# Moving block loads between issuing queues in a one-layer encoder kernel: staged weight blocks to the sync engine, f loads to GpSimd

## The chip, the core and the metric

One core of a Trainium2 chip runs the whole layer. The metric is device time in microseconds (us) of one execution. A core has TensorE (PE), VectorE (DVE), ScalarE (ACT), GpSimd (POOL) and the sync engine (SP). SP, ACT and POOL can each issue DMAs; each works its program strictly in order, so a wait holds back everything that stands behind it on that engine.

## What is computed

The layer has one combined input projection, three token mixers, a gated merge, an output projection and a squared-ReLU MLP, all in float32 (SEQ 512, D_MODEL 2048):

```python
h = _rmsnorm(x, norm1[l])
proj = jnp.einsum('bsd,de->bse', h, w_in[l])
(u_pool, c_b, c_c, c_x, q, k, v, qi, ki, wi, gate_logits) = jnp.split(proj, pts, axis=-1)
...
merged = (g[:, :, 0] * jnp.einsum('bsp,pd->bsd', a, w_pool_out[l])
          + g[:, :, 1] * jnp.einsum('bsp,pd->bsd', bconv, w_conv_out[l])
          + g[:, :, 2] * jnp.einsum('bsp,pd->bsd', c, w_attn_out[l]))
x = x + jnp.einsum('bsd,de->bse', merged, w_o[l])
h2 = _rmsnorm(x, norm2[l])
f = jnp.square(jax.nn.relu(jnp.einsum('bsd,df->bsf', h2, w_ff1[l])))
x = x + jnp.einsum('bsf,fd->bsd', f, w_ff2[l])
```

## The kernel before

Every float32 operand is split into a high part (rounded, made by ACT) and a low part (the rest, made by DVE), and a product is three matmuls: hi*hi, hi*lo, lo*hi. For the narrow weights the piece of work is a **unit**: 2 tiles of 128 rows by 256 columns. SP loads two units at a time into `w_raw` (512 KB, `load`, L535), ACT makes `w_hi` (`split_hi`, L458), DVE makes `w_lo` (`split_lo`, L465), PE multiplies (L488 to L490, for v L974 to L976). `w_hi` and `w_lo` have four slots, and the splits run three units ahead of PE (`PREFETCH`): turn n of DVE's and ACT's loop handles unit n + 3, whose slot is free when PE has finished unit n - 1.

The order is q and k (64 units, 8 per pass), v (32 units), then the attention with the convolution's weights (48 units). In these stretches something else is prepared on the side: for three large products later on (the gate's first column block, `J` 0, and the output projection's, `J` 6 and 7) Strassen-like sums of weight blocks are needed. A **stage** s (12 of them) loads four 512 KB blocks into `stage` (L2736), DVE mixes them with four subtractions (`mix_stage`, L1960, L1963, L1966, L1969), and each mixed block is stored to `t_dram` (L2741), to be read back later as `block_g` or `block_w`. Stages 0 to 7 share one set of four buffers, stages 8 to 11 another. GpSimd issues both the loads and the stores. It waits for the previous stage's stores to land before it issues the next stage's loads:

```python
if s:
    pool.wait_ge(stage_mixed, 4 * s)
    pool.wait_ge(stage_stored, 64 * s)
```

DVE does the mixes between its splits at fixed turns: in q and k at turns 4 to 7 of each pass of 8 (mixes 0, 1, 2, 3), in v at turns 11 to 14, 18 to 21 and 25 to 28 (stages 8, 9, 10), and stage 11 at turns 3 to 6 of the attention. Mix 0 waits until all four blocks have landed, and the splits of later units stand behind it on DVE.

The MLP's first product is computed 16 times over (`q`, 0 to 15), its squared results f are split and stored by SP to `f_dram` (L768, 256 KB each). The second product (`J` 8 to 15, two passes over each of four chunks of f; 28 turns a pass, its weights loaded by SP as `group`, L600) reads f back into `sf`: `load_s(c, n, freed)` (L1762) waits for the chunk's stores and for PE's last use of the buffer, then issues two 1 MB loads from ACT's queue. ACT's list calls it 28 times, between the splits and evictions that ACT also does.

Of the kernel before, what the change touches and what calls it, by code (L numbers as in the profile page):

```python
# [29 lines left out]
F32 = mybir.dt.float32  # L30
# [32 lines left out]
def build(nc, xT, x, cst_dram, w_in, pool_w, w_po, w_co, w_ao, w_o, w_f1, w_f2, out):  # L63
# [31 lines left out]
    with ctx:  # L95
# [432 lines left out]
        def _(sp):  # L528
# [29 lines left out]
                            sp.dma_start(h_dram[k0:k0 + 4].rearrange("k p c -> p k c"), xin[:, k0:k0 + 4, :]  # L558
                                         ).then_inc(h_spilled, 16)

            with sp.Fori(0, 8) as i:
                for n in range(LP):
                    load(i * LP + (u_qk // 2 + n), n % RAWS, w_in, n * 2 * UK * P, i * COLS + c_q)
            with sp.Fori(0, 4) as i:
                for n in range(LP):
                    load(i * LP + (u_v // 2 + n), n % RAWS, w_in, n * 2 * UK * P, i * COLS + c_v)
            sp.wait_ge(a_lo, NW)
            for hl, part in ((0, br_hi), (1, br_lo)):
                sp.dma_start(br_dram[0:4, hl].rearrange("k p c -> p k c"), part[:, 0:4, :].bitcast(F32)
# [8 lines left out]
            def spill_c(h):  # L578
                sp.wait_ge(c_lo, h + 1)
                for hl, part in ((0, br_hi), (1, br_lo)):  # L580
                    sp.dma_start(br_dram[8 + h, hl], part[:, 8 + h, :].bitcast(F32)).then_inc(c_spilled, 16)
# [38 lines left out]
            for i, col in enumerate((c_c, c_x, c_b, c_c + COLS, c_x + COLS, c_b + COLS)):  # L620
                for n in range(LP):
                    load(u_att // 2 + i * LP + n, n % RAWS, w_in, n * 2 * UK * P, col)
                    l = i * LP + n
                    if l >= 7 and (l - 7) % 3 == 0:
                        spill_c((l - 7) // 3)
                    if l == 15:
                        sp.wait_ge(ab_spilled, 32)
                        for idx in range(4):
                            load_block(0, idx)
                    if l == 17:  # L630
                        spill_b(0)
            spill_c(6)
            sp.wait_ge(pv_mm, ATTN_HEADS)

# [618 lines left out]
        def _(act):  # L1253
# [499 lines left out]
                if q < F1_PAIRS and k == 13:  # L1753
                    square_f(q, 0)

            def load_s(c, n, freed):

                for s in range(PIECES):
                    act.wait_ge(f_spilled[s], 32 * ((28 * (c + 1) - s + PIECES - 1) // PIECES))
                act.wait_ge(g_done, freed)  # L1760
                for h in range(2):
                    act.dma_start(sf[h][n].rearrange("p l k c -> p l (k c)").bitcast(F32),  # L1762
                                  f_dram[c, n, :, :, h * 2 * S:(h + 1) * 2 * S].rearrange("l p c -> p l c")
                                  ).then_inc(s_landed[n], 16)


            hi1(0, 0, 0)
            hi1(0, 1, 0)
# [25 lines left out]
            for q in range(1, F1_PAIRS):  # L1794
                for k in range(14):
                    hi1(q, k // 2, k % 2)
                    act_after(q, k)
                    if q == F1_PAIRS - 1 and k in (5, 7, 9, 11, 13):
                        n = (k - 5) // 2
                        load_s(0, n, 28 * 8 + 14 * q + 2 * n + 2)  # L1800

            for J in range(8, 16):
                it, c = J - 8, (J - 8) // 2
                for idx, (n, g) in enumerate(order_of(J)):
                    hi2(J, n, g)
                    if it == 0 and idx < 14:
                        act_after(F1_PAIRS, idx)
                    if it == 0 and idx in (1, 3):
                        load_s(0, 5 + idx // 2, K2 - 3 + idx)
                    if it % 2 == 1 and c < 3 and idx == 11:  # L1810
                        load_s(c + 1, 0, K2 + 28 * it + 8)
                        load_s(c + 1, 1, K2 + 28 * it + 8)
                    if it % 2 == 1 and c < 3 and idx == 23:
                        for n in (4, 3, 2):
                            load_s(c + 1, n, K2 + 28 * it + 20)
                    if it % 2 == 0 and c and idx == 3:
                        load_s(c, 5, K2 + 28 * it)
                        load_s(c, 6, K2 + 28 * it)


        @block.vector
        def _(dve):
# [149 lines left out]
            for n in range(8 * UP):  # L1972
                split_lo(dve, u_qk + n + PREFETCH, n + PREFETCH)
                if n == 0:
                    pool_group(3)
                if n % UP < 6:
                    t = n % UP % 3
                    chain.step(dve.max(top8[t], work[t][:]))
                    chain.wait()
                    chain.step(dve.match_replace(work[t][:], top8[t], work[t][:], EMPTY))  # L1980
                    chain.wait()
                if n % UP >= 4:
                    mix_stage(n // UP, n % UP - 4)


            def mask(t):
# [20 lines left out]
            for n in range(4 * UP):  # L2007
# [28 lines left out]
                    chain.wait()  # L2036
                if n == 24:
                    diagonals(dve, rqk, 32, dk)
                if 11 <= n < 29 and (n - 11) % 7 < 4:
                    mix_stage(8 + (n - 11) // 7, (n - 11) % 7)  # L2040


            def landed(J, place):
# [662 lines left out]
        @block.gpsimd  # L2706
        def _(pool):

            for kt in range(KT):
                pool.wait_ge(x_squared, kt + 1)  # L2710
                if kt == 0:
                    pool.tensor_copy(dg[:, :], sq[:, 0]).then_inc(x_summed, 1)
                else:
                    pool.wait_ge(x_summed, kt)
                    pool.tensor_tensor(dg[:, :], dg[:, :], sq[:, kt % 2], ALU.add).then_inc(x_summed, 1)


            for kt in range(1, KT, 2):
                pool.wait_ge(h_hi, kt + 1)
                pool.tensor_tensor(act_lo[:, kt, :], xin[:, kt, :], act_hi[:, kt, :].bitcast(F32),  # L2720
                                   ALU.subtract).then_inc(h_lo_odd, 1)

            for s in range(12):
                J, g, h = (0, 6, 7)[s // 4], s % 4, s // 8
                w, c0 = (w_in, c_gate) if J == 0 else (w_o, (J - 6) * S)
                if s == 0:
                    pool.wait_ge(score_added, 24)
                    pool.wait_ge(score_mm, 24)
                if s == 8:
                    pool.wait_ge(topk_done, 1)  # L2730
                if s:
                    pool.wait_ge(stage_mixed, 4 * s)
                    pool.wait_ge(stage_stored, 64 * s)
                for b in range(4):
                    r0, col = (b // 2) * (D // 2) + 2 * g * P, c0 + b % 2 * (D // 2)
                    pool.dma_start(stage[h][b][:], w[r0:r0 + 2 * P, col:col + S].rearrange("(k p) c -> p k c", p=P)  # L2736
                                   ).then_inc(stage_landed, 16)
                for i, b in enumerate((0, 1, 3, 2)):
                    kind = (0, 2, 1, 3)[i]
                    pool.wait_ge(stage_mixed, 4 * s + i + 1)  # L2740
                    pool.dma_start(t_dram[s // 4, kind, g].rearrange("p (k c) -> p k c", k=2), stage[h][b][:]  # L2741
                                   ).then_inc(stage_stored, 16)


def constants(norm1, norm2, pool_scale, conv_w, q_gain, k_gain):
# [32 lines left out]
```

## Time and profile before

| | us |
|---|---|
| runs | 2750.91, 2757.0, 2753.04 |
| median | 2753.04 |
| the profiled execution, its own time | 2753.44 |
| its span, first to last instruction | 2751.6 |
| PE busy in the span | 2666.3 |
| DVE busy | 2013.1 |
| ACT busy | 1232.1 |
| GpSimd busy | 98.5 |

Between the span and the execution's own time lie 1.8 us. PE's busy time is modelled from pipelined matmuls, so 97% busy does not say that PE runs at its best; the gaps between the starts of matmuls do. [...]

### The profile page before, as it was taken

The page shows a single profiled execution, that of the slowest core. Times are in us where ns is not written, and L with a number is a line of the kernel's source. Part 1 is how long each engine was busy: PE and PEld are TensorE (multiplying, and loading weights), DVE is VectorE, ACT ScalarE, POOL GpSimd, SP SyncE. Part 2 cuts the span into 40 slices and gives each one's busy share as a digit, 9 for nine tenths or more (in the row PEclk, how much of TensorE's full clock was granted, in tenths as well). Part 3 has the DMA queues.
Part 4 walks back from the last instruction along what each step waited for, and adds up shares of the span by engine and source line. Part 5 has one row for each costly group of instructions (what it writes and reads, how often), then busy time and mean ns, then how long its engine had stood idle before and what let it go on. Part 6 is the DMA issues. An engine that isn't in the chain of part 4 may idle for free.

```text
span 2751.6 us, 37283 instructions
## 1 busy us (share of the span) xinstructions
PE 2666.3 (97%) x14614; PEld 2304.4 (84%) x14614; DVE 2013.1 (73%) x2347; ACT 1232.1 (45%) x1591; POOL 98.5 (4%) x124
## 2 busy tenths in 40 slices
PE   7998999999999999999998999999999899999998
PEld 6686798777888888888888999999998788888887
DVE  8575644546777777556777888888887788888787
ACT  5322232334544444234465666566565333333332
POOL 4011111000000000000000000000000000000000
PEclk9999999999999999999999999999999999999999
DMA  4476757435655446745673655665668667675843
GB/s 138 155 232 211 252 176 253 134 119 202 226 169 162 153 158 199 263 158 199 222 245 108 215 178 183 215 203 173 215 211 322 242 241 269 210 291 168 312 151 109
DMA packets 313272, 552.98 MB, mean 201 GB/s; under 512 B 19536, under 2 KB 134864, under 8 KB 313104
## 3 DMA queue, kind: packets, MB, share of 16 engines
q1 hardware_dynamic: 276352, 426.82, 47.0%
q10 hardware_dynamic: 22928, 73.54, 7.1%
q0 software_dynamic: 13824, 50.34, 5.4%
q8 instruction: 111, 1.82, 0.3%
q14 instruction: 57, 0.47, 0.0%
HBM read 433.05 MB, written 117.44 MB: 200 GB/s over the span
## 4 chain that ended last, share of the span: by engine, by line
PE 77%; DVE 9%; DMA 8%; issue 4%; ACT 1%; POOL 1%; SPq 0%; ACTq 0%; DVEq 0%; POOLq 0%
PE main L1231 7%; PE main L1232 7%; PE main L1233 7%; PE aux L1129 7%; PE aux L1131 7%; PE aux L1130 7%; PE main L1129 5%; PE main L1131 5%; PE main L1130 5%; DMA group<-w_ff 3%; PE main L488 3%; PE main L490 2%; PE main L489 2%; DMA t_dram<-stage 2%; DVE f_wl L2051 1%
## 5 line engine op out<-in xcount | busy, mean ns | idle before, releaser
L1231 PE MATMUL main<-sf,f_wh 128*128 128x256 f32 x1728 | 491.7, 285 | 9.7 <-DVE cf_low L2537 6.0
L1232 PE MATMUL main<-sf,f_wh 128*128 128x256 f32 x1728 | 491.4, 284 | 0.0
L1233 PE MATMUL main<-sf,f_wl 128*128 128x256 f32 x1728 | 491.3, 284 | 0.0
L1231 PEld LDWEIGHTS main<-sf,f_wh 128*128 128x128 f32 x1728 | 333.9, 193 | 10.1 <-DVE cf_low L2537 6.2
L1232 PEld LDWEIGHTS main<-sf,f_wh 128*128 128x128 f32 x1728 | 333.8, 193 | 0.0
L1233 PEld LDWEIGHTS main<-sf,f_wl 128*128 128x128 f32 x1728 | 333.8, 193 | 0.0
L458 ACT ACTIVATE w_hi<-w_raw 128x512 fp32r<-128x512 f32 (+1 forms) x184 | 113.1, 616 | 330.1 <-PE main L490 240.0
L488 PE MATMUL main<-act_hi,w_hi 128*128 128x512 f32 (+1 forms) x528 | 216.9, 411 | 23.2 <-DVE w_lo L465 23.2
L465 DVE TENSOR_TENSOR w_lo<-w_raw,w_hi 128x512 fp32r<-128x512 f32 (+1 forms) x184 | 129.7, 708 | 148.4 <-ACT w_hi L458 146.6
L1418 ACT ACTIVATE f_wh<-group 128x1024 fp32r<-128x1024 f32 x128 | 135.6, 1061 | 217.3 <-PE aux L1131 87.0
L1129 PE MATMUL aux<-f_wh,sf 128*128 128x512 f32 x512 | 201.2, 393 | 10.3 <-DVE f_wl L2051 5.7
L490 PE MATMUL main<-act_hi,w_lo 128*128 128x512 f32 (+1 forms) x528 | 209.0, 396 | 0.0
L489 PE MATMUL main<-act_lo,w_hi 128*128 128x512 f32 (+1 forms) x528 | 208.6, 395 | 0.0
L2051 DVE TENSOR_TENSOR f_wl<-group,f_wh 128x1024 fp32r<-128x1024 f32 x128 | 156.5, 1222 | 65.5 <-ACT f_wh L1418 64.8
L2509 DVE TENSOR_TENSOR f_wl<-f1raw,f_wh 128x1024 fp32r<-128x1024 f32 x128 | 156.4, 1223 | 61.5 <-ACT f_wh L1690 61.5
L1130 PE MATMUL aux<-f_wl,sf 128*128 128x512 f32 x512 | 200.5, 392 | 0.0
L1131 PE MATMUL aux<-f_wh,sf 128*128 128x512 f32 x512 | 200.4, 391 | 0.0
L1690 ACT ACTIVATE f_wh<-f1raw 128x1024 fp32r<-128x1024 f32 x128 | 135.2, 1057 | 108.9 <-PE main L1233 108.5
L1418 ACT ACTIVATE f_wh<-f2x 128x1024 fp32r<-128x1024 f32 x96 | 102.0, 1062 | 157.4 <-PE aux L1131 77.3
L2051 DVE TENSOR_TENSOR g_wl<-group_g,g_wh 128x1024 fp32r<-128x1024 f32 x80 | 98.0, 1225 | 74.1 <-ACT g_wh L1418 74.1
L1129 PE MATMUL main<-f_wh,sf 128*128 128x512 f32 x384 | 149.8, 390 | 0.0
L1130 PE MATMUL main<-f_wl,sf 128*128 128x512 f32 x384 | 149.6, 390 | 0.0
(285 smaller groups left out, 6182.1 us busy)
## 6 DMA issues: line engine op xcount, KB each, us to landing
group<-w_ff SPq DMA_DIRECT2D x160, 512.0 KB, 5.0
f1raw<-w_ff SPq DMA_DIRECT2D x128, 512.0 KB, 5.8
sf<-f_dram ACTq DMA_DIRECT2D x56, 1024.0 KB, 11.9
group_g<-w_in SPq DMA_DIRECT2D x100, 512.0 KB, 4.5
w_raw<-w_in SPq DMA_DIRECT2D x88, 512.0 KB, 4.7
f_dram<-piece_hi SPq DMA_DIRECT2D x112, 256.0 KB, 4.0
f_dram<-piece_lo SPq DMA_DIRECT2D x112, 256.0 KB, 5.2
t_dram<-stage POOLq DMA_DIRECT2D x48, 512.0 KB, 3.9
```

The lines of the kernel that those rows point to most:

```text
L488: pe.matmul(out, wh, hi[:, kt, :], start=(kt == last_kt[0]), stop=False)
L489: pe.matmul(out, wh, lo[:, kt, :], start=False, stop=False)
L490: mm = pe.matmul(out, wl, hi[:, kt, :], start=False, stop=(kt == last_kt[1]))
L1129: pe.matmul(part, sh, wh, start=first, stop=False, skip_group_check=True)
L1130: pe.matmul(part, sh, wl, start=False, stop=False, skip_group_check=True)
L1131: mm = pe.matmul(part, sl, wh, start=False, stop=last, skip_group_check=True)
L1231: pe.matmul(part, hi_at(8, k)[:, cols], sh, start=first, stop=False, skip_group_check=True)
L1232: pe.matmul(part, hi_at(8, k)[:, cols], sl, start=False, stop=False, skip_group_check=True)
L1233: mm = pe.matmul(part, lo_at(8, k)[:, cols], sh, start=False, stop=last, skip_group_check=True)
L1418: act.activation(hi_at(J, k_of(J, n, g))[:], source_of(J, n, g).rearrange("p k c -> p (k c)"), ACT.Copy).then_inc(f_hi, 1)
L2051: dve.tensor_tensor(lo_at(J, k)[:], source_of(J, n, g).rearrange("p k c -> p (k c)"), hi_at(J, k)[:].bitcast(F32), ALU.subtract).then_inc( ...
L2509: dve.tensor_tensor(lo_at(8, k)[:], f1_source(q, n, h).rearrange("p k c -> p (k c)"), hi_at(8, k)[:].bitcast(F32), ALU.subtract).then_inc( ...
```

## The change

1. The stage loads move from GpSimd's program to SP's (`load_stage`), between the `w_raw` loads: in q and k after every fourth one, in v after loads 2, 8 and 13 (stages 7, 8, 9), in the attention after loads 1 and 4 (stages 10, 11). The waits go with them. GpSimd keeps the stores. SP's two hardware loops over q, k and over v are written out for that.
2. DVE's mixes move: in q and k mix 0 to turn 5, mix 1 to turn 6, mixes 2 and 3 both to turn 7; in v to turns 9 to 12, 17 to 20 and 25 to 28.
3. The 56 f loads (`load_s`) move from ACT's list to the end of GpSimd's, same order of buffers and same waits.

```diff
-            with sp.Fori(0, 8) as i:
-                for n in range(LP):
-                    load(i * LP + (u_qk // 2 + n), n % RAWS, w_in, n * 2 * UK * P, i * COLS + c_q)
-            with sp.Fori(0, 4) as i:
-                for n in range(LP):
-                    load(i * LP + (u_v // 2 + n), n % RAWS, w_in, n * 2 * UK * P, i * COLS + c_v)
+            def load_stage(s):
+
+                J, g, h = (0, 6, 7)[s // 4], s % 4, s // 8
+                w, c0 = (w_in, c_gate) if J == 0 else (w_o, (J - 6) * S)
+                if s == 0:
+                    sp.wait_ge(score_added, 24)
+                    sp.wait_ge(score_mm, 24)
+                else:
+                    sp.wait_ge(stage_mixed, 4 * s)
+                    sp.wait_ge(stage_stored, 64 * s)
+                if s == 8:
+                    sp.wait_ge(topk_done, 1)
+                for b in range(4):
+                    r0, col = (b // 2) * (D // 2) + 2 * g * P, c0 + b % 2 * (D // 2)
+                    sp.dma_start(stage[h][b][:], w[r0:r0 + 2 * P, col:col + S].rearrange("(k p) c -> p k c", p=P)
+                                 ).then_inc(stage_landed, 16)
+
+            for l in range(8 * LP):
+                load(u_qk // 2 + l, l % RAWS, w_in, l % LP * 2 * UK * P, l // LP * COLS + c_q)
+                if l >= 6 and (l - 6) % LP == 0:
+                    load_stage((l - 6) // LP)
+            for l in range(4 * LP):
+                load(u_v // 2 + l, l % RAWS, w_in, l % LP * 2 * UK * P, l // LP * COLS + c_v)
+                if l == 2:
+                    load_stage(7)
+                if l == 8:
+                    load_stage(8)
+                if l == 13:
+                    load_stage(9)
...
+                    if l in (1, 4):
+                        load_stage(10 + l // 4)
...
-                if n % UP >= 4:
-                    mix_stage(n // UP, n % UP - 4)
+                if n % UP >= 5:
+                    mix_stage(n // UP, n % UP - 5)
+                if n % UP == UP - 1:
+                    mix_stage(n // UP, 3)
...
-                if 11 <= n < 29 and (n - 11) % 7 < 4:
-                    mix_stage(8 + (n - 11) // 7, (n - 11) % 7)
+                if n % 8 in (1, 2, 3, 4) and 8 < n:
+                    mix_stage(8 + n // 8 - 1, n % 8 - 1)
...
+            def load_s(c, n, freed):
+
+                for s in range(PIECES):
+                    pool.wait_ge(f_spilled[s], 32 * ((28 * (c + 1) - s + PIECES - 1) // PIECES))
+                pool.wait_ge(g_done, freed)
+                for h in range(2):
+                    pool.dma_start(sf[h][n].rearrange("p l k c -> p l (k c)").bitcast(F32),
+                                   f_dram[c, n, :, :, h * 2 * S:(h + 1) * 2 * S].rearrange("l p c -> p l c")
+                                   ).then_inc(s_landed[n], 16)
+
+            for n in range(7):
+                load_s(0, n, 28 * 8 + 14 * (F1_PAIRS - 1) + 2 * n + 2)
+            for c in range(1, 4):
+                it = 2 * c - 1
+                for n in (0, 1):
+                    load_s(c, n, K2 + 28 * it + 8)
+                for n in (4, 3, 2):
+                    load_s(c, n, K2 + 28 * it + 20)
+                for n in (5, 6):
+                    load_s(c, n, K2 + 28 * it + 28)
```

What stands in a row on the engines. First DVE in the second half of one q/k pass, before (`MAX` and `MATCH_REPLACE` are the top-k selection that runs on the side):

```order
L465 TENSOR_TENSOR w_lo<-w_raw,w_hi 128x512
L1978 MAX st<-work_64 128x8
L1980 MATCH_REPLACE work_64<-st,work_64 128x384
L1960 TENSOR_TENSOR stage_0_103<-stage_1_104,stage_0_103 128x1024
L465 TENSOR_TENSOR w_lo<-w_raw,w_hi 128x512
L1978 MAX st<-work_65 128x8
L1980 MATCH_REPLACE work_65<-st,work_65 128x512
L1963 TENSOR_TENSOR stage_1_104<-stage_3_106,stage_1_104 128x1024
L465 TENSOR_TENSOR w_lo<-w_raw,w_hi 128x512
L1966 TENSOR_TENSOR stage_3_106<-stage_3_106,stage_0_103 128x1024
L465 TENSOR_TENSOR w_lo<-w_raw,w_hi 128x512
L1969 TENSOR_TENSOR stage_2_105<-stage_2_105,stage_3_106 128x1024
```

And the same place with the change:

```order
L465 TENSOR_TENSOR w_lo<-w_raw,w_hi 128x512
L1979 MAX st<-work_65 128x8
L1981 MATCH_REPLACE work_65<-st,work_65 128x512
L1961 TENSOR_TENSOR stage_0_103<-stage_1_104,stage_0_103 128x1024
L465 TENSOR_TENSOR w_lo<-w_raw,w_hi 128x512
L1964 TENSOR_TENSOR stage_1_104<-stage_3_106,stage_1_104 128x1024
L465 TENSOR_TENSOR w_lo<-w_raw,w_hi 128x512
L1967 TENSOR_TENSOR stage_3_106<-stage_3_106,stage_0_103 128x1024
L1970 TENSOR_TENSOR stage_2_105<-stage_2_105,stage_3_106 128x1024
```

Mix 0 stands one turn later, and the last two mixes follow each other without a split between them.

SP in the end of v and the beginning of the attention, with the change (the second set of buffers is 107 to 110; before, this queue held the `w_raw` and `br_dram` rows alone):

```order
L535 DMA w_raw<-w_in 128x4x256 x2
L592 DMA br_dram<-br_hi 128x4x512
L592 DMA br_dram<-br_lo 128x4x512
L535 DMA w_raw<-w_in 128x4x256 x2
L575 DMA stage_0_107<-w_o 128x2x512
L575 DMA stage_1_108<-w_o 128x2x512
L575 DMA stage_2_109<-w_o 128x2x512
L575 DMA stage_3_110<-w_o 128x2x512
L535 DMA w_raw<-w_in 128x4x256 x3
```

The four loads of stage 10 now stand behind the two 1 MB stores to `br_dram` and two `w_raw` loads, and three more `w_raw` loads stand behind them.

## Rows read from the trace of the kernel before

**Rows 1.** The page, part 1: busy us (share of the span) xinstructions.

```profile
PE 2666.3 (97%) x14614; PEld 2304.4 (84%) x14614; DVE 2013.1 (73%) x2347; ACT 1232.1 (45%) x1591; POOL 98.5 (4%) x124
```

**Rows 2.** Busy time by stretch; at the end granted clock, DMA share, GB/s.

```profile
139.80:344.80 205.00, 186.01 (x781) 150.55 (x780) 132.24 (x250) 49.79 (x81) 38.64 (x60) 0.96 0.70 233
...
2080.00:2150.00 70.00, 58.32 (x362) 53.40 (x361) 44.38 (x49) 31.18 (x39) 0.00 (x0) 0.91 1.02 393
```

**Rows 3.** Timeline of PE: start us, us, engine, line, op, [idle before <-releaser].

```profile
139.84 0.39 PE L488 MATMUL main<-act_hi,w_hi 128*128 128x512 f32 x1
142.56 0.39 PE L488 MATMUL main<-act_hi,w_hi 128*128 128x512 f32 x1
...
348.80 0.55 PE L974 MATMUL main<-w_hi,act_hi 128*128 128x256 f32 x1 [3.84 <-DVE w_lo L465]
353.04 0.95 PE L503 MATMUL aux<-cst,sq 128*128 128x1 f32 x8
...
421.86 0.68 PE L974 MATMUL main<-w_hi,act_hi 128*128 128x256 f32 x1
424.06 0.28 PE L974 MATMUL main<-w_hi,act_hi 128*128 128x256 f32 x1
426.94 0.28 PE L974 MATMUL main<-w_hi,act_hi 128*128 128x256 f32 x1
456.06 0.58 PE L974 MATMUL main<-w_hi,act_hi 128*128 128x256 f32 x1 [4.85 <-DVE w_lo L465]
467.78 0.40 PE L488 MATMUL main<-act_hi,w_hi 128*128 128x512 f32 x1
```

**Rows 4.** Timeline of DVE and PE: two of DVE's waits, and PE's behind them.

```profile
184.75 1.23 DVE L1960 TENSOR_TENSOR stage<-stage,stage 128x1024 f32<-128x1024 f32 x1 [6.80 <-DMA stage<-w_in]
186.64 0.50 PE L488 MATMUL main<-act_hi,w_hi 128*128 128x512 f32 x1 [0.39 <-DVE w_lo L465]
212.64 1.23 DVE L1960 TENSOR_TENSOR stage<-stage,stage 128x1024 f32<-128x1024 f32 x1 [11.05 <-DMA stage<-w_in]
214.52 0.79 PE L488 MATMUL main<-act_hi,w_hi 128*128 128x512 f32 x1 [5.29 <-DVE w_lo L465]
```

**Rows 5.** The chain of waits in order of time, one round of a stage.

```profile
219.46 1.15 DVE stage L1969
220.89 6.18 DMA t_dram<-stage
227.77 2.19 POOL stage L2736 x3
229.96 6.43 issue
236.38 4.22 DMA stage<-w_in
240.70 1.23 DVE stage L1960
```

**Rows 6.** Issues by line in 1266 to 1276 us: KB each, us to landing.

```profile
mt<-x SPq DMA_DIRECT2D x4, 512.0 KB, 5.8
```

**Rows 7.** Timeline of SP: the issue of these four loads.

```profile
1266.48 1.90 SPq L693 DMA_DIRECT2D mt<-x  x4
```

**Rows 8.** Chain of waits, the store of stage 9.

```profile
431.07 8.53 DMA t_dram<-stage
```

**Rows 9.** DMA queues and issues in 2080 to 2150 us.

```profile
q10 hardware_dynamic: 3752, 14.45, 53.5%
q1 hardware_dynamic: 6899, 12.98, 48.5%
...
sf<-f_dram ACTq DMA_DIRECT2D x12, 1024.0 KB, 13.1
group<-w_ff SPq DMA_DIRECT2D x13, 512.0 KB, 13.3
```

**Rows 10.** Timeline of ACT's DMA queue: the largest group of f loads.

```profile
2415.28 4.34 ACTq L1762 DMA_DIRECT2D sf<-f_dram  x6
```

More of the change, by code:

```diff
@@ L1754, in act_after @@
                     square_f(q, 0)
[L1756 to L1764, printed above, removed]
             hi1(0, 0, 0)
@@ L1797, in _ @@
                     act_after(q, k)
-                    if q == F1_PAIRS - 1 and k in (5, 7, 9, 11, 13):
-                        n = (k - 5) // 2
-                        load_s(0, n, 28 * 8 + 14 * q + 2 * n + 2)
             for J in range(8, 16):
@@ L1807, in _ @@
                         act_after(F1_PAIRS, idx)
[L1808 to L1818, printed above, removed]
         @block.vector
@@ L2723, in _ @@
             for s in range(12):
[L2724 to L2737, printed above, removed]
+                g, h = s % 4, s // 8
                 for i, b in enumerate((0, 1, 3, 2)):
```

## The prediction

> **What bounds the kernel now.** I read the page first, then busy time by stretch, then the starts of PE's matmuls, the waits, and the chain. The page gives PE as busy for 97% of the span [rows 1], so time can only come from the gaps in PE's work. The table by stretch shows where they are: from 139.8 to 344.8 us (q and k) PE is busy for 186.0 of 205.0 us, and at 2080 to 2150 us for 58.3 of 70 [rows 2]. The starts of matmuls give the exact loss. One unit takes 142.56 - 139.84 = 2.72 us at full clock [rows 3], so the 64 units of q and k need 174.1 us and v should start at 313.9. It starts at 348.80, behind DVE: **34.9 us lost**. Its first unit, at the lower clock level that followed the idle time, takes 353.04 - 348.80 = 4.24 us where 24 matmuls take 426.94 - 424.06 = 2.88: 1.4 us more. The last 13 units of v and one small step of 0.5 us should take 37.9 us; they take 467.78 - 421.86 = 45.9, with a gap before 456.06 [rows 3]: **8.0 us lost**. Together 44.3 us.
>
> The waits say why. DVE sits before mix 0 of a stage until the loads have landed, and the splits stand behind it. A wait of 6.80 us cost PE 0.39 us, one of 11.05 us cost 5.29 [rows 4]: the three units split ahead cover about 6 us, and what is beyond comes out of PE. The chain shows one round of a stage [rows 5], from mix 0 at 212.64 [rows 4] to the next at 240.70: four mixes with splits and selection between them, 8.0 us; 0.3 to the last store's issue; its landing, 6.2, and 0.7 until GpSimd goes on; three load issues, 2.2; 6.4 in which the fourth is not issued; its landing, 4.2. The sum is 28.1 us, where PE needs 8 x 2.72 = 21.8 for the pass. The round sets the pace, not PE.
>
> **The stage loads.** GpSimd spends from 227.77 to 236.38, 8.6 us, on issuing four loads [rows 5]. The gap before the fourth looks like a limit of three loads in flight on its queue, since it ends about one landing after the first. VectorE is no reason for it: it stood idle through the gap (the chain resumes on DVE at 240.70). SP issued four equal loads in 1.90 us, and each landed 5.8 us after its issue [rows 6, 7], so the last lands some 1.4 + 5.8 = 7.2 us after the first issue. One 512 KB `w_raw` load stands just ahead of them; at the 393 GB/s of the fullest stretch [rows 2] it adds 1.3: 8.5 us. The lower bound is 7.2; the upper is the landing in that fullest stretch, 13.3 [rows 9], plus 1.4: 14.7. I take 8.5, since the loads stand in much the same company as in rows 6.
>
> [...]
>
> **The mixes.** In the new order the selection and one split lie ahead of mix 0 or behind mix 3, and no longer between: the 8.0 us from mix 0 to the end of mix 3 become about 6.0, an estimate (a split and a selection less, some 2 us). New round: 6.0 + 0.3 + 6.2 + 0.1 + 8.5 = **21.1 us against 21.8**. So PE sets the pace again, narrowly. Even a round of 22.6 would cost DVE 0.8 x 7 = 6 us over the seven rounds, which the units ahead cover. SP's place fits: the load after which it turns to a stage can go out when DVE has made turn 8s + 2, mix 0 stands at turn 8s + 5 behind its split and selection, 3 x 2.72 + some 1.2 = 9.4 us later, and 8.5 are needed. The previous stage's stores (last mix at turn 8s - 1, about 2.9 us into it, plus 0.3 + 6.2) land 9.4 us after that turn began, 1.2 us into turn 8s + 2: SP hardly waits. While it waits, later `w_raw` loads stand behind it, but the next one is due only some seven turns (19 us) after it could go, so that costs nothing. If this cover were gone (a wait of over 19 us) PE would lose all beyond it.
>
> **In v** the turns are less even. Stage 9 is loaded at turn 16 and mixed at turn 17: DVE waits some 4 us, covered. Stage 10 is the tightest. Its loads stand behind SP's two 1 MB stores, and behind the stores of stage 9, which took 8.5 us to land in that company [rows 8]. Counting from turn 16: stage 9 mixed at 17.5, stored at 26.3, `w_raw` at turn 24 (27.0), stage 10 landed at about 34.5; mix 0 stands at about 29.9. DVE waits 4.6 us, under the 6 of cover. Each us beyond that is lost, so I leave 1 us of the 8.0.
>
> **The f loads.** ACT spends up to 4.34 us of its queue on six issues [rows 10], but ACT is 45% busy [rows 1]. In 2080 to 2150 us the DMA share is 1.02 at 393 GB/s [rows 2]: the f loads' queue holds 53.5% and SP's 48.5% [rows 9]. That stretch is short of DMA bandwidth, and the bytes stay the same. GpSimd issues the same loads at the same releases, with at most three in flight. I cost the move at 0, between two bounds: all 11.7 us that PE lacks there [rows 2] gone, or as much again lost. [...]
>
> **Sum.** The profiled execution took 2753.4 us, 0.4 above the median, so the two can be used alike. 2753.4 - 34.9 - 1.4 - 8.0 + 1.0 + 0 = 2710.1: **2710 us**. A measurement of this kernel can tell about 0.2%, 5.5 us, from no change.
>
> **Rivals.**
> (A) *The stage loads stay late, for bandwidth.* The same bytes per round in 21.8 instead of 26.8 us (the mean round, as 34.9 / 7 + 21.8) raise the DMA share from 0.70 [rows 2] to 0.86. If the four land in 12 us, the round is 24.6 and DVE loses 2.8 x 7 = 20, less 6 of cover: 14 us come back, 2724. At the bound of 14.7, (27.3 - 21.8) x 7 - 6 = 32 come back and v's 7 too: 2749. For it: the share; against it: DMA has slack in every pass, and a load's latency before was set by its issue.
> (B) *The f stretch gains too.* ACT no longer stands in line with its DMA waits, SP's stores and `group` loads get more of the DMA engines while GpSimd's queue is limited to three. Up to 11.7 us: 2698 to 2705. For it: landings of 13.3 us [rows 9] are what ACT and DVE wait for there. Against: the bytes.
> (C) *Slower than before: GpSimd's queue is too thin for f.* Six 1 MB loads (buffers 4, 3, 2) are released at turn 20 of a pass and needed at turn 8 of the next, 16 x 2.72 = 43.5 us later. Three in flight at 13.1 us [rows 9] make 26 us: in time. From 21.8 us a landing they are late. At 30 us they take 60, 16.5 late, in each of four chunks: 66 us lost, 2776. The gap of 6.4 us before a fourth load [rows 5] speaks for it, the landings against it. [...]
> (D) *It doesn't do what it says:* SP is held by a stage's stores longer than the weights' 19 us, so PE waits for `w_raw` instead. The gain is given back in part: at 5 us a pass in seven passes, 2745.
>
> **How the numbers follow.** Forecast 0.70, A 0.12, B 0.09, C 0.04, D 0.05. The range goes from B's middle (2701) to a little beyond A's first value (2728). The forecast, B and most of A and D are faster by over 5.5 us: 0.93. Same: 0.03, the ends of A and D. Slower: 0.04, C.
>
> **What would show it.** Right: v's first unit near 314 us; DVE's waits before mix 0 under 6 us; PE's idle time behind DVE's `w_lo` in q, k, v under 3 us; the clock at 1.00 there; the attention from about 424; rounds of 21.8. Wrong: rounds of over 23 us, a store-to-mix time of over 10 us (A), PE or ACT waiting for `w_raw` (D), PE waiting for `sf` (C), or 2080 to 2150, moved by the gain, much changed (B).

## The result, and the profile after

| | before | changed |
|---|---|---|
| median of the runs, us | 2754.19 | 2714.65 (2708.92 to 2717.85, 4 runs) |
| ratio | | 0.9855, 95% interval 0.9832 to 0.9877 |
| the profiled execution, its own time | 2753.44 | 2711.86 |

The forecast of 2710 us, 2701 to 2728, holds: the change takes 39.5 us off. Two of its terms were too large, though, and what it put at nothing or did not count made up for them. To see that, the gain is laid out over the program by the starts of PE's first matmuls, as in [rows 3] (us):

| | before | changed | gain in the stretch before |
|---|---|---|---|
| v starts | 348.80 | 316.88 | 31.9 |
| attention starts | 467.78 | 433.91 | 2.0 |
| MLP's first product starts | 1453.82 | 1420.34 | -0.4 |
| second product starts | 2119.83 | 2082.59 | 3.8 |
| last matmul | 2743.69 | 2702.14 | 4.3 |

The page, parts 1 and 4 (busy us and share; the chain by engine), against [rows 1]:

```profile
PE 2654.4 (98%) x14614; PEld 2297.0 (85%) x14614; DVE 2013.1 (74%) x2347; ACT 1231.9 (45%) x1591; POOL 102.3 (4%) x132
...
PE 89%; DVE 5%; DMA 3%; ACT 1%; issue 1%; SPq 1%; DVEq 0%; ACTq 0%
```

Busy time by stretch, for q and k, the middle of v, and chunk 0 of the MLP (columns as in [rows 2]: length, then PE, PEld, DVE, ACT, POOL, TensorE's granted clock with 1.00 for full speed, DMA share, GB/s):

```profile
139.80:314.00 174.20, 174.20 (x769) 143.68 (x768) 134.82 (x254) 49.21 (x80) 15.11 (x28) 1.00 0.80 271
387.00:424.00 37.00, 32.90 (x255) 31.83 (x253) 15.88 (x28) 9.19 (x15) 2.16 (x5) 0.95 0.69 238
2046.00:2116.00 70.00, 60.25 (x382) 54.80 (x382) 51.50 (x59) 32.36 (x41) 8.54 (x13) 0.95 1.02 390
```

In q and k PE is never idle and the clock is 1.00: nothing is left there. In v PE lacks 4.1 of 37 us. VectorE's waits before mix 0 (timeline of DVE; three of the eight in q and k, which are 3.0 to 5.9 us, the third with mix 3 of its stage; then stage 9 and stage 10) and PE's starts and gaps behind them (timeline of PE):

```profile
164.20 1.22 DVE L1961 TENSOR_TENSOR stage<-stage,stage 128x1024 f32<-128x1024 f32 x1 [2.97 <-DMA stage<-w_in]
208.47 1.23 DVE L1961 TENSOR_TENSOR stage<-stage,stage 128x1024 f32<-128x1024 f32 x1 [5.92 <-DMA stage<-w_in]
229.99 1.23 DVE L1961 TENSOR_TENSOR stage<-stage,stage 128x1024 f32<-128x1024 f32 x1 [4.57 <-DMA stage<-w_in]
...
234.72 1.23 DVE L1970 TENSOR_TENSOR stage<-stage,stage 128x1024 f32<-128x1024 f32 x1
...
388.97 1.23 DVE L1961 TENSOR_TENSOR stage<-stage,stage 128x1024 f32<-128x1024 f32 x1 [5.71 <-DMA stage<-w_o]
390.72 0.74 DVE L2025 SCALAR_TENSOR_TENSOR br_lo<-aux,cst,br_hi 128x512 fp32r<-128x512 f32 x1
422.45 1.23 DVE L1961 TENSOR_TENSOR stage<-stage,stage 128x1024 f32<-128x1024 f32 x1 [9.56 <-DMA stage<-w_o]
```

```profile
316.88 0.28 PE L999 MATMUL main<-w_hi,act_hi 128*128 128x256 f32 x1
...
391.52 1.36 PE L987 MATMUL aux<-poolT,poolw 128*128 128x512 f32 x2 [3.05 <-DVE br_lo L2025]
424.33 0.39 PE L999 MATMUL main<-w_hi,act_hi 128*128 128x256 f32 x1 [1.38 <-DVE w_lo L465]
433.91 0.40 PE L488 MATMUL main<-act_hi,w_hi 128*128 128x512 f32 x1
```

None of the waits of up to 5.92 us in q and k reached PE. The 5.71 us of stage 9 did, and not through a weight split: behind mix 0 stands `br_lo` of the pool mixer, and PE's pool matmul waits for it. VectorE makes this `br_lo` at turn 18 of v, and PE needs it at unit 19, so that path is about one unit ahead and not three: 5.71 - 3.05 = 2.7 us. The wait of 9.56 us for stage 10 cost 1.38.

Where SP turns to a stage in v and the attention (timeline of SP: stages 8, 9, the `br_dram` stores, stage 10), and what SP waited for in 139 to 314 us (us in total, times, longest):

```profile
340.82 2.44 SPq L575 DMA_DIRECT2D stage<-w_o  x4
...
379.54 2.10 SPq L575 DMA_DIRECT2D stage<-w_o  x4
...
399.18 0.37 SPq L592 DMA_DIRECT2D br_dram<-br_hi  x1
399.59 0.51 SPq L592 DMA_DIRECT2D br_dram<-br_lo  x1
...
411.70 2.44 SPq L575 DMA_DIRECT2D stage<-w_o  x4
```

```profile
SPq L535 <- DVE w_lo L465: 125.9, 28, 9.4
SPq L570 <- DMA t_dram<-stage: 15.8, 7, 5.5
```

DMA queues and issues in 139 to 314 us:

```profile
stage<-w_in SPq DMA_DIRECT2D x16, 512.0 KB, 6.2
stage<-w_o SPq DMA_DIRECT2D x16, 512.0 KB, 6.1
```

And around the beginning of chunk 0, 2046 to 2116 us, with PE's three gaps there, and last the first of them as it was in the kernel before (against [rows 2, 9]):

```profile
q0 software_dynamic: 3808, 14.68, 54.9%
q1 hardware_dynamic: 6678, 12.59, 47.1%
...
sf<-f_dram POOLq DMA_DIRECT2D x13, 1024.0 KB, 10.1
group<-w_ff SPq DMA_DIRECT2D x14, 512.0 KB, 13.4
```

```profile
2075.39 0.58 PE L1256 MATMUL main<-sf,f_wh 128*128 128x256 f32 x1 [2.77 <-DVE cf_low L2540]
2103.92 0.50 PE L1154 MATMUL aux<-f_wh,sf 128*128 128x512 f32 x1 [2.10 <-DVE f_wl L2054]
2114.53 0.80 PE L1154 MATMUL aux<-f_wh,sf 128*128 128x512 f32 x1 [4.87 <-DVE yb L2659]
```

```profile
2112.08 0.58 PE L1231 MATMUL main<-sf,f_wh 128*128 128x256 f32 x1 [5.96 <-DVE cf_low L2537]
```

The stretch is as short of bandwidth as before, 390 against 393 GB/s; the f loads land in 10.1 us instead of 13.1, `group` loads in 13.4 as before (13.3), and the stores to `f_dram` later than before (medians 10.7 and 12.6 us against 8.8 and 9.9).

### The profile page after: what moved, and what is told of

Its sections match the earlier page's. It is cut to its first block, busy times and chain, and to the rows that moved or that the text cites. A ratio compares the mean times of both kernels' runs of the same rounds, so it can differ in the third digit from the quotient of the medians.

```text
span 2710.1 us, 37111 instructions
## 1 busy us (share of the span) xinstructions
PE 2654.4 (98%) x14614; PEld 2297.0 (85%) x14614; DVE 2013.1 (74%) x2347; ACT 1231.9 (45%) x1591; POOL 102.3 (4%) x132
## 4 chain that ended last, share of the span: by engine, by line
PE 89%; DVE 5%; DMA 3%; ACT 1%; issue 1%; SPq 1%; DVEq 0%; ACTq 0%
PE aux L1154 8%; PE aux L1155 8%; PE aux L1156 8%; PE main L1256 8%; PE main L1258 8%; PE main L1257 8%; PE main L1154 6%; PE main L1155 6%; PE main L1156 6%; PE main L488 5%; PE main L490 5%; PE main L489 5%; DMA group<-w_ff 1%; PE main L1187 1%; PE aux L1187 1%; PE aux L1189 1%
```

## The experiments

All times are medians; ratios are to the kernel before, run on the same chip beside them (2753.2 to 2754.2 us), each with its 95% interval. "v starts" and the like are PE's first matmuls in the profiled execution; they vary with what comes before q and k: q and k themselves begin between 140.7 and 144.4 us (by ACT's eviction of the pass before).

### The changed kernel again, and its two halves

> The changed kernel once more, beside the others on this chip. Both theories: 2709 to 2718 us, the attention's first unit at about 434 us.

2718.0 us, 0.9870 (0.9856 to 0.9884); v starts at 316.91. The gain and its place repeat. One thing does not: the gap before the pool matmul is there again, 3.07 us, but the clock stays at 1.00 behind it, where the first execution had 0.95 in the same 37 us (0.61 from 391.5 to 395), and v lasts 115.5 us instead of 117.0. So the fall of the clock is no fixed part of what the gap costs. The row of `again` for 387 to 424 us, columns as above:

```profile
387.00:424.00 37.00, 32.58 (x264) 31.69 (x263) 17.37 (x30) 9.19 (x15) 2.67 (x5) 1.00 0.70 244
```

`stage_only` keeps parts 1 and 2 of the change and leaves the f loads in ACT's list; `f_only` makes part 3 alone.

```diff
 stage_only, ACT's list (as in the kernel before)
+                    if q == F1_PAIRS - 1 and k in (5, 7, 9, 11, 13):
+                        n = (k - 5) // 2
+                        load_s(0, n, 28 * 8 + 14 * q + 2 * n + 2)
...
 f_only, end of GpSimd's list (and none in ACT's)
+            for n in range(7):
+                load_s(0, n, 28 * 8 + 14 * (F1_PAIRS - 1) + 2 * n + 2)
...
```

> The stage loads and the mixes as changed, the f loads left on ACT. Theory 1 (the f loads' move is worth about 8 us by itself, and the staging about 34): the attention starts at 434 us as with the whole change, and the time is 8 us above it, about 2722. Theory 2 (the f loads' move is worth nothing, as the prediction had it, and the 8 us come from how the later work happened to fall): within 3 us of the whole change, 2712 to 2718.

> Only the f loads moved to GpSimd, stages as before. Theory 1: about 2746 us, 8 under the kernel before, the gain all after 2080 us. Theory 2: 2751 to 2757. The attention starts at 468 us by both.

`stage_only`: 2719.27 us, 0.9879 (0.9865 to 0.9893), 1.3 us over `again`, less than the intervals tell apart. `f_only`: 2750.3 us, 0.9986 (0.9975 to 0.9996), so 3.9 us faster (1.1 to 6.9), below what was called telling in the forecast, and on the side of a gain. All but a few us come from the stage part.

Where the f loads' part sits shows in the time from the first to the second product's first matmul, over all traces of this study: with the f loads on ACT 666.0 (before), 668.0, 666.0, 667.9 and 666.0, mean 666.8; on GpSimd 662.3 (changed), 663.7, 662.5, 664.1, 662.5, 664.4, 662.7 and 666.8, mean 663.6. That is some 3.2 us, with one trace of eight outside. Its place is PE's wait for `cf_low` in the last turns of the first product, some 7 us before the second begins: 5.8 to 6.5 us with the f loads on ACT, 2.6 to 3.3 on GpSimd, and 5.2 in the one outside, `v9_10`. From the second product to the last matmul the traces give 622.8 to 627.1 us with the loads on ACT and 619.5 to 629.7 on GpSimd, so the 4.3 us of the table above are no part of the change.

### The gap before the fourth load

`before_ring` is the kernel before with the constant `dynamic_dma_scratch_size` at 2048 instead of 1024 (and the small tile `norm` 512 bytes lower).

```diff
-    nc = bacc.Bacc("TRN2", target_bir_lowering=False, num_devices=1, dynamic_dma_scratch_size=1024)
+    nc = bacc.Bacc("TRN2", target_bir_lowering=False, num_devices=1, dynamic_dma_scratch_size=2048)
```

> [...] If the 6.4 us before the fourth stage load are a limit on loads in flight, the gap goes, a round falls from 28 to about 22 us, v starts at 317 to 325 us instead of 349, and the time is 2722 to 2732. If the gap is what GpSimd needs to write descriptors, nothing changes: 2751 to 2757.

2726.48 us, 0.9908 (0.9893 to 0.9922); v starts at 328.59. One constant gives 27.7 us, 20.2 of them up to v's start and 7.0 in v, which lasts 112.0 us instead of 119.0. The time is as expected, v's start 3.6 us later than that: a round takes 23.9 us on average and not 22. Its timeline of POOL:

```profile
197.13 2.97 POOL L2736 DMA_DIRECT2D stage<-w_in  x4 [6.24 <-DMA t_dram<-stage]
...
221.01 2.96 POOL L2736 DMA_DIRECT2D stage<-w_in  x4 [5.44 <-DMA t_dram<-stage]
```

Four issues in one row of 3.0 us, where [rows 5] had three, then 6.43 us, then the fourth: the 6.43 us were no time that GpSimd needs for an issue. So the limit in flight goes with this constant, by its name the size of a scratch memory for DMA; what is kept there, and where it lies, no run shows. What is left before the loads is the landing of the last store, 6.24 and 5.44 us of GpSimd's idle time in these two rows.

### Loads' queue against mixes' turns

`sp_oldturns` is the changed kernel with the mixes at the turns of before; `pool_newturns` is the kernel before with the mixes at the new turns and nothing else.

```diff
 pool_newturns against the kernel before (sp_oldturns: the reverse, against the changed one)
-                if n % UP >= 4:
-                    mix_stage(n // UP, n % UP - 4)
+                if n % UP >= 5:
+                    mix_stage(n // UP, n % UP - 5)
+                if n % UP == UP - 1:
+                    mix_stage(n // UP, 3)
...
-                if 11 <= n < 29 and (n - 11) % 7 < 4:
-                    mix_stage(8 + (n - 11) // 7, (n - 11) % 7)
+                if n % 8 in (1, 2, 3, 4) and 8 < n:
+                    mix_stage(8 + n // 8 - 1, n % 8 - 1)
```

> The changed kernel with DVE's mixes at their old turns (4 to 7; in v from 11, 18 and 25). Theory 1 (the place of the mixes matters): mix 0 one turn earlier adds 2.7 us and the selection behind it to DVE's wait, 4 to 6 us become 7 to 9, beyond the cover of 6; PE loses 1 to 3 us in each of eight passes, 2726 to 2742 in all. Theory 2 (a round of under 21.8 us is all that counts, the turns only shift it): v starts at 317 to 319, within 3 us of the changed kernel.

> Part 2 of the change alone: the stage loads stay on GpSimd, behind their stores, and only VectorE's mixes move to the new turns (5, 6, 7, 7 of a round's eight instead of 4, 5, 6, 7). Theory 1 (the round of the kernel before is a ring: load, four mixes, store, load; the new turns take one unit of some 2.7 us out of the mixes' part, and the limit on loads in flight stays): a round shrinks from some 26.3 us to 24 to 25, v starts at 330 to 342 instead of 348.80, and the time is 2734 to 2748 us. Theory 2 (the queue alone sets the round, the turns only matter once loads are on the sync engine): v starts within 2 us of 348.80 and the time is 2750 to 2757. A third: since loads come late here, putting two mixes into one unit delays the splits and v starts later than 348.80.

`sp_oldturns`: 2726.0 us, 0.9902 (0.9886 to 0.9918), v starts at 330.5 (and q and k 1.6 us later than before). VectorE waits 4.7 to 7.4 us at mix 0 in q and k. `pool_newturns`: 2734.54 us, 0.9928 (0.9916 to 0.9940), v starts at 329.1. Its timelines of POOL, DVE and PE, one round:

```profile
197.92 2.19 POOL L2738 DMA_DIRECT2D stage<-w_in  x3 [5.81 <-issue]
206.50 0.72 POOL L2738 DMA_DIRECT2D stage<-w_in  x1 [6.39 <-issue]
```

```profile
210.51 1.23 DVE L1960 TENSOR_TENSOR stage<-stage,stage 128x1024 f32<-128x1024 f32 x1 [7.84 <-DMA stage<-w_in]
...
234.42 1.23 DVE L1960 TENSOR_TENSOR stage<-stage,stage 128x1024 f32<-128x1024 f32 x1 [6.96 <-DMA stage<-w_in]
```

```profile
212.39 0.50 PE L488 MATMUL main<-act_hi,w_hi 128*128 128x512 f32 x1 [1.70 <-DVE w_lo L465]
...
236.30 0.50 PE L488 MATMUL main<-act_hi,w_hi 128*128 128x512 f32 x1 [1.84 <-DVE w_lo L465]
```

The gap before the fourth load is still there, and yet the round is 234.42 - 210.51 = 23.9 us (24.5 on average over the seven, against 26.8 before). A ring of load, mixes and stores gets shorter when any of its links does. Each of three edits alone takes about the same from q and k: the turns 19.7 us of v's start, the constant 20.2, the queue 18.3, or 19.9 counted from where q and k begin (with the new turns the wait of stage 7 falls in v and costs 1.76 us there). They do not add up, since 32 us is all there is to get.

`sp_oldturns` shows one thing more, about v. There the change's own new turns do harm: with the old ones v lasts 112.1 us, with the new ones 117.0 and 115.5. At the old turn 18 mix 0 of stage 9 stands behind the `br_lo` that PE needs next, at the new turn 17 ahead of it. In `sp_oldturns` VectorE waits 2.03 us there, and PE's pool matmul not at all:

```profile
399.71 0.75 DVE L2023 SCALAR_TENSOR_TENSOR br_lo<-aux,cst,br_hi 128x512 fp32r<-128x512 f32 x1
402.49 1.23 DVE L1961 TENSOR_TENSOR stage<-stage,stage 128x1024 f32<-128x1024 f32 x1 [2.03 <-DMA stage<-w_o]
```

### How much of a late load VectorE's lead covers

`late` is the changed kernel with the loads of stages 0 to 7 behind the next `w_raw` load.

```diff
-                if l >= 6 and (l - 6) % LP == 0:
-                    load_stage((l - 6) // LP)
+                if l >= 7 and (l - 7) % LP == 0:
+                    load_stage((l - 7) // LP)
...
-                if l == 2:
+                if l == 3:
                     load_stage(7)
```

> The changed kernel with each stage load of q, k and early v issued one raw weight load later on the sync engine (after load 7 of each four instead of 6, and stage 7 after load 3 of v), 5.4 us later. It shows how much of a late landing VectorE's lead covers. Theory 1 (cover of some three units, 8 us, as the forecast has it): VectorE's waits before a stage's first mix rise from 3.0 to 5.9 us to some 8.4 to 11.3, TensorE loses only what is over 8 us, that is 0 to 3 us a round, v starts at 320 to 338 instead of 316.9 and the time is 2718 to 2736. Theory 2 (there is hardly any slack left behind the 4 to 6 us that VectorE waits now): TensorE loses nearly all of the added 5.4 us a round, v starts at 350 or later, and the time is 2748 or more. Theory 3 (VectorE does not arrive early at all, since its waits stretch its own round): v starts within 1 us of 316.9 and the time stays at 2714.

2733.79 us, 0.9922 (0.9909 to 0.9935); v starts at 331.3. Two of its rounds, DVE and PE:

```profile
216.15 1.22 DVE L1961 TENSOR_TENSOR stage<-stage,stage 128x1024 f32<-128x1024 f32 x1 [7.61 <-DMA stage<-w_in]
...
239.74 1.23 DVE L1961 TENSOR_TENSOR stage<-stage,stage 128x1024 f32<-128x1024 f32 x1 [6.64 <-DMA stage<-w_in]
```

```profile
218.03 0.50 PE L488 MATMUL main<-act_hi,w_hi 128*128 128x512 f32 x1 [2.47 <-DVE w_lo L465]
...
241.62 0.50 PE L488 MATMUL main<-act_hi,w_hi 128*128 128x512 f32 x1 [1.49 <-DVE w_lo L465]
```

The size that theory 1 gave came out, but not its working. Waits of 6.1 to 7.6 us (not 8.4 to 11.3) cost PE 1.0 to 3.3 each: the cover is some 5 us here, not 8. That the waits are shorter than expected because PE's lost time gives the loads more room is likely, not shown. The cover is no fixed number: in `v9_10` a wait of 6.15 us in q and k cost nothing. The changed kernel's waits of up to 5.9 us are near the edge all the same: 5.4 us later costs 14.4 us at v's start, and the median is 15.8 to 19.1 us above those of the changed kernel. In `v_fix` below, which leaves q and k as they are, one wait came out at 7.12 us and cost PE 0.98.

### What v kept back

`v9` is the changed kernel with stage 9's loads one `w_raw` load earlier. `v_fix` adds that SP's two `br_dram` stores go out after stage 11's loads. `v9_10` is `v9` with stage 10's loads after the attention's load 0.

```diff
 v9
-                if l == 13:
+                if l == 12:
                     load_stage(9)
 v_fix also: the stores at L592, with their wait, from behind v's loop to attention load 5
 v9_10 also
-                    if l in (1, 4):
+                    if l in (0, 4):
                         load_stage(10 + l // 4)
```

> The changed kernel with stage 9's loads one w_raw load earlier (after load 12 of v, not 13). Theory 1 (DVE's wait of 5.7 us before stage 9's mix 0 keeps the pool's matmul waiting on DVE's br_lo, with less cover than a split has): the 3.2 us gap of PE at 388 us and the low clock behind it go, the attention starts at about 428 instead of 433, the time is about 2713. Theory 2 (the gap there comes from the pool's own chain ACT to DVE to PE): nothing changes, 2715 to 2719.

> As the one before, and the two 1 MB stores to br_dram moved from ahead of stage 10's loads to behind stage 11's. Theory 1 (these stores lengthen the landing of stage 9's stores and of stage 10's loads, and so DVE's wait of 9.6 us): that wait falls under 6 us, PE's 1.5 us gap at 422 us goes, the attention starts at about 426.5, the time is about 2711. Theory 2 (the wait comes from SP's late turn to stage 10 alone): the wait stays at 8 us or more, and the time is that of the run before.

> v9 with stage 10 loaded one raw weight load earlier too (attention's load 0 instead of 1), some 5 us earlier. Theory 1 (stage 10's late turn at the sync engine is what VectorE's 9.4 us wait and TensorE's last gap of 1.4 us in v come from): the wait falls to 3 to 5 us, the gap goes, attention starts 1 to 2.5 us earlier than in v9 (426.9), at 424.5 to 426, and the time is 2709 to 2712. Theory 2 (the load then waits at the sync engine for the stores of stage 9, which lie in the same buffer, and raw weight loads wait behind it): the wait falls by less than 2 us, and the time is 2712 to 2716.

`v9`: 2712.56 us, 0.9850 (0.9837 to 0.9864); v lasts 112.05 us instead of 117.03 or 115.5, and PE's gap at the pool matmul and VectorE's wait for stage 9 are gone. `v_fix`: 2714.75 us, 0.9862 (0.9847 to 0.9877); v lasts 112.3 (its time is above that of `v9` for another reason: PE lost 1.4 us in q and k) and the wait for stage 10 is still 9.68 us, so the stores ahead of these loads were not what kept them; the turn at which SP comes to them was. `v9_10`: 2708.82 us, 0.9837 (0.9824 to 0.9850). Stage 10's row in `v9` and in `v9_10`, and v's whole stretch in the latter:

```profile
415.44 1.22 DVE L1961 TENSOR_TENSOR stage<-stage,stage 128x1024 f32<-128x1024 f32 x1 [9.40 <-DMA stage<-w_o]
```

```profile
411.72 1.23 DVE L1961 TENSOR_TENSOR stage<-stage,stage 128x1024 f32<-128x1024 f32 x1 [4.39 <-DMA stage<-w_o]
```

```profile
314.00:427.00 113.00, 113.00 (x919) 110.04 (x918) 57.48 (x93) 35.69 (x63) 8.56 (x16) 1.00 0.69 231
```

PE is without a gap from 139.8 to 427.0 us, and v lasts 110.6 us. This is the lowest median of the study, but its interval overlaps that of the changed kernel: that it beats it is likely and not shown.

### The two cheap edits together, with no load moved

`after_ring` is the changed kernel with the constant at 2048; `pool_new_ring` is the kernel before with the new turns and the constant at 2048, and no load changes its engine.

```diff
-    nc = bacc.Bacc("TRN2", target_bir_lowering=False, num_devices=1, dynamic_dma_scratch_size=1024)
+    nc = bacc.Bacc("TRN2", target_bir_lowering=False, num_devices=1, dynamic_dma_scratch_size=2048)
 and for pool_new_ring the diff of pool_newturns
```

> [...] Theory 1 (the limit of three keeps the DMA engines free for SP's stores and loads at the first chunk, and that is the small gain of the f part): the stretch from the MLP's first to its second product grows from 663 back to 666 to 668 us, PE's gap in the first product's last turns from 2.9 to 6 us, the time from 2718 to 2721 or 2722. Theory 2 (it is ACT, freed of waits and issues, that gains): 663 us and 2.9 us as they are, 2715 to 2719.

> [...] Alone, the turns gave 19.0 us and shortened a round to 24.1 us, and the memory gave 26.7 us. Theory 1 (moving the loads to the sync engine does nothing by itself in q and k, it only gets rid of the gap before the fourth load): the round would be some 24.1 - 5.6 = 18.5 us, under the 21.8 that TensorE needs, so v starts at 315 to 319, v lasts 110 to 114 us, and the time is 2712 to 2721 us, the f loads being still on ScalarE. Theory 2 (the sync engine's place also starts the loads earlier, because GpSimd's load stands behind the landing of the last store and its own slower issue, 3.0 us against 1.9): v starts at 322 or later and the time is 2722 or more.

`after_ring`: 2717.54 us, 0.9868 (0.9853 to 0.9883), no gain. VectorE's waits in q and k fall to between 0.7 and 3.5 us, but they were covered already. The largest group of f loads on POOL in the changed kernel and in `after_ring`:

```profile
2223.80 2.10 POOL L2740 DMA_DIRECT2D sf<-f_dram  x3 [22.07 <-PE aux L1156]
2235.52 1.40 POOL L2740 DMA_DIRECT2D sf<-f_dram  x2 [9.62 <-issue]
```

```profile
2225.54 4.20 POOL L2740 DMA_DIRECT2D sf<-f_dram  x6 [29.84 <-PE aux L1156]
```

These six land in 14.0 us (median), so all six were in flight at once. The f loads, no longer held to three, land later, in 14.1 us instead of 10.1 between 2046 and 2116 us, and over the page as well: the page's issue rows of the changed kernel and of `after_ring`,

```profile
sf<-f_dram POOLq DMA_DIRECT2D x56, 1024.0 KB, 9.7
```

```profile
sf<-f_dram POOLq DMA_DIRECT2D x56, 1024.0 KB, 12.7
```

and from first to second product it takes 667.6 us, as with the f loads on ACT (11.9 us a landing), and PE waits 7.06 us for `cf_low`. So an ACT freed of the f loads is not enough for the 3.2 us. That fits the limit as their reason, but it is one trace, and `v9_10` had 666.8 with the limit. Nor does the way fit that was expected, that the limit leaves the DMA engines to SP: with it `group` loads land no sooner (13.4 us against 13.6 in `after_ring`) and the `f_dram` stores later (10.7 and 12.6 us against 7.0 and 9.2). It stays open.

`pool_new_ring`: 2711.35 us, 0.9850 (0.9833 to 0.9866); v starts at 314.7 (q and k 1.9 us earlier than before). Busy time in q and k, and one round on POOL and DVE:

```profile
139.80:314.00 174.20, 174.20 (x770) 144.26 (x769) 137.03 (x253) 49.19 (x80) 37.25 (x59) 1.00 0.81 274
```

```profile
213.01 2.95 POOL L2738 DMA_DIRECT2D stage<-w_in  x4 [4.59 <-DMA t_dram<-stage]
```

```profile
223.00 1.23 DVE L1960 TENSOR_TENSOR stage<-stage,stage 128x1024 f32<-128x1024 f32 x1 [0.44 <-DMA stage<-w_in]
```

VectorE waits 2.2 us at most in q and k. (The text above takes 26.7 and 19.0 us for what the constant, its "memory", and the turns gave alone; the medians give 27.7 and 19.2.) The loads on GpSimd, behind the stores' landing, come early enough once the gap is gone and mix 0 stands a unit later. v lasts 110.6 us, as in `v9_10`. With no load moved the time is that of the changed kernel.

## Why the prediction was right, and where not

- **What bounds q and k: right.** The ring of load, mixes and stores set the pace, not PE: PE went from 186.0 of 205.0 us busy [rows 2] to 174.20 of 174.20, at clock 1.00.
- **The 34.9 us of q and k: one unit too large.** PE is never idle up to v's start at 316.88. Counting back 174.1 us puts q and k's first unit at 142.8. The forecast took the row at 139.84 [rows 3] for it; it is the unit before, and the row at 142.56 is the right one (ACT begins to evict the pass before at 142.76, when PE is done with it). So v should have been forecast for 316.7, the loss was 32.1, and 31.9 came back.
- **The limit of three loads in flight: right**, shown by `before_ring`: with the constant at 2048 four loads go out in 2.97 us. The forecast did not name the constant as its cause.
- **The new round, 21.1 against 21.8: the sum was a little short, the verdict held.** The rounds from mix 0 to mix 0 took 20.3 to 24.0 us, 21.7 on average. From SP's first issue of a stage to its mix 0 it took 8.0 to 10.3 us, on average 9.1, where 8.5 stood (landings of 6.2 us against 5.8). "SP hardly waits" was wrong: it waited for the stores of the stage before in all seven rounds, 15.8 us in total and 5.5 at most. So was the place of mix 0, "9.4 us later": VectorE stood there 2.1 to 6.4 us after SP's first issue (the mix's start less its wait), on average 4.6, and waited 3.0 to 5.9 us instead of about none. SP's waits explain 2.3 us a round of the difference; what else brought VectorE there early is not shown. The cover of "about 6 us" from [rows 4] carried it: 5.9 us cost nothing here, in `late` 6.1 us cost 1.0, in `v9_10` 6.15 nothing.
- **The mixes, 8.0 to 6.0 us: right.** From mix 0 at 229.99 to the end of mix 3 at 235.95 it takes 6.0 us, and in `pool_newturns` the average round is 2.3 us shorter than before. But the turns alone do as much for v's start as the queue alone, which the prediction treated as the main part.
- **v, 1.4 + 8.0 - 1.0 = 8.4 us: the term that failed.** Only 2.0 came back. (The 1.4 is v's first unit in the kernel before, at a clock of 0.65 from 348.80 to 353.04 us.) The step "stage 9: DVE waits some 4 us, covered" failed twice: the wait was 5.71, and the cover was counted in weight units, while `br_lo` stood behind the mix with only 2.7 us until PE's pool matmul needed it. That cost 3.05 us, and the clock of 0.95 in 387 to 424 us another 0.05 x 37 = 1.9, an estimate (in `again`, at clock 1.00, v was 1.5 us shorter). "Stage 10: 4.6 us" was 9.56, and cost 1.38. Together 6.3 us, and the changed kernel's v is 117.03 - 110.6 = 6.4 us longer than that of `v9_10`, which has none of them. The forecast's own 118.98 - 8.4 = 110.6 us for v is just what can be had, by luck: it had taken 1.4 + 8.0 = 9.4 us as lost and kept back 1 for stage 10, but its 37.9 us for the last 13 units were short. `v9_10`, without a gap, takes 426.72 - 388.04 = 38.7 for them.
- **The f loads, 0: mis-sized by some 3 to 4 us.** `f_only` measured 3.9 (1.1 to 6.9), and the traces put some 3.2 us of it at PE's wait for `cf_low` before the second product. The bounds of 11.7 us either way held. The forecast's 0 rested on the bytes, which stay the same; the landings did not stay: they fell from 11.9 to 9.7 us over the page with the queue, and were 12.7 in `after_ring`. What made the time shorter stays open.
- **Rivals.** A (whose 14 and 32 us that "come back" are losses that return): the four loads took 8.0 to 10.3 us and not 12, though the DMA share rose to 0.80. B came in a third of its size, and not in its way: SP's `group` loads and `f_dram` stores landed no sooner. C: the f loads were in time with three in flight, PE has no wait for `sf`. D: SP was held up to 5.5 us in q and k, far from 19.
- **The signs.** In q and k they came as given: the clock at 1.00, rounds of 21.7 us, waits under 6. In v they did not: a wait of 9.56 us, a gap of 3.05, a clock of 0.95, and the attention at 433.9 instead of 424.
- **The sum.** Against the profiled execution: 3.0 too much for q and k and 6.4 too much for v, 9.4 us; 3.8 not counted for f, and 4.3 of plain scatter behind it, 8.1; and 0.4 lost in the attention and what follows. 2710.1 + 9.4 - 8.1 + 0.4 = 2711.8, measured 2711.86. That it came so near is luck: terms that were too large, one put at nothing and scatter of the other sign made it look better than its working was.

## What to carry to other kernels

Where a side job runs as a ring (load, work, store, wait, load), write down the ring's length and the main engine's period, and shorten the cheapest link: here two cheap edits (two lines of turns, one constant) did what moving 48 loads to another engine did, and past the period nothing more is gained. When a wait is called covered, look at everything that stands behind it on its engine and ask for each item how far ahead it runs; the one with the least lead (here a small pool mixer step, 2.7 us ahead) decides. A gap in front of the fourth load on GpSimd's DMA queue, 6.43 us in this kernel, was gone with `dynamic_dma_scratch_size` at 2048, without a change of the schedule: where such a gap stands, the constant is the cheaper thing to try.

## What the runs showed that was not expected

- `dynamic_dma_scratch_size` at 2048 instead of 1024: 27.7 us less (0.9908), with nothing else changed but the place of `norm`. The same limit probably held back one of GpSimd's stores in the changed kernel too: the last store of stage 1 at 194.56 us stood 4.57 us with nothing to wait for, and SP's next stage loads waited for its landing. With the constant at 2048 (`after_ring`) that gap is gone. But two like it, 4.38 and 4.54 us before stores at 238.16 and 430.79 us, are as long with 2048 (4.63 us, the last row, and 4.50 at 428.74), so not every such gap is the constant's, and the cause of these stays open.

```profile
194.56 0.54 POOL L2731 DMA_DIRECT2D t_dram<-stage  x1 [4.57 <-issue]
...
200.47 1.92 SPq L575 DMA_DIRECT2D stage<-w_in  x4
```

```profile
234.38 1.07 POOL L2731 DMA_DIRECT2D t_dram<-stage  x2 [4.63 <-issue]
```

- Landings were shorter with the limit in flight: at DMA shares of 1.02 and 1.01 in 2046 to 2116 us, the 1 MB f loads landed in 10.1 us with the constant at 1024 and in 14.1 at 2048. The time did not show it: 2714.65 and 2718.0 us against 2717.54.
- Equal waits have unequal prices: 5.92 us at 208.47 cost PE nothing, 5.71 us at 388.97 cost 3.05. And equal gaps have unequal prices: behind 3.05 us the clock fell to 0.61 for 3.5 us, behind 3.07 us in `again` it stayed at 1.00.
